# The chunk loop of a state space scan: chunks pipelined on TensorE, the skip term and the column terms of the decays as matmuls

## The reference

```python
xdt = x * dt
acs = cumsum(dt * a_neg)                       # within a chunk of 128 tokens
seg = acs[t] - acs[s]
decay_in = exp(where(tri, seg, NEG_INF))
cb = einsum('bctgn,bcsgn->bctsg', cc, bc)
y_diag = einsum('bctsg,bctsgh,bcsghp->bctghp', cb, decay_in, xdt)
states = einsum('bcsgn,bcsgh,bcsghp->bcghpn', bc, decay_out, xdt)
...
y_off = einsum('bctgn,bcghpn,bctgh->bctghp', cc, prev, exp(acs))
...
y = y_fwd + y_bwd + d_skip * xs
y = y * silu(z)
```

## Time and profile before

| | us |
|---|---|
| median of 3 runs | 2483.04 (2482.91 to 2487.15) |
| the profiled execution | 2485.22 |
| its span (first to last instruction) | 2483.4 |
| TensorE matmuls busy | 2426.9 (98%) |
| VectorE busy | 1375.8 (55%) |
| ScalarE busy | 998.4 (40%) |
| GpSimd busy | 1263.1 (51%) |

### The profile page before, as it was taken

The page is one execution under the profiler, slowest core; times in us unless marked ns, Lnnn a source line. Parts: engine busy times, 40 slices in busy tenths (PEclk is TensorE's granted clock), DMA queues, the critical chain, the costliest instruction groups (busy, mean ns, idle before and its releaser), DMA issues.

```text
span 2483.4 us, 33046 instructions
## 1 busy us (share of the span) xinstructions
PE 2426.9 (98%) x12882; PEld 2072.2 (83%) x12882; DVE 1375.8 (55%) x1561; ACT 998.4 (40%) x1737; POOL 1263.1 (51%) x814
## 2 busy tenths in 40 slices
PE   7999999999999999999999999998999999999999
PEld 6989997887888888887898899977878888888887
DVE  4476557738655546428345765586385555544332
ACT  4345567613444344212024465585144344431110
POOL 3242113323977877666633311142349877866664
PEclk9999999999999999999999999999999999999999
DMA  4434444231222212654333334442212222226544
GB/s 160 136 114 125 134 139 149 81 119 68 85 79 91 85 68 85 217 178 132 130 121 94 110 128 151 134 136 90 89 64 102 85 70 100 83 90 201 174 141 142
DMA packets 102964, 290.68 MB, mean 117 GB/s; under 512 B 7800, under 2 KB 30328, under 8 KB 101112
## 3 DMA queue, kind: packets, MB, share of 16 engines
q1 hardware_dynamic: 80360, 255.73, 30.4%
q10 hardware_dynamic: 22456, 32.90, 4.1%
HBM read 229.84 MB, written 58.75 MB: 116 GB/s over the span
## 4 chain that ended last, share of the span: by engine, by line
PE 81%; DVE 9%; ACT 4%; POOL 3%; issue 2%; DMA 1%; SPq 0%; ACTq 0%; DVEq 0%; POOLq 0%
PE PS L690 20%; PE PS L694 20%; PE PS L693 20%; PE PS L775 3%; PE PS L779 3%; PE PS L778 3%; PE PS L945 2%; PE PS L934 2%; POOL WL L629 2%; DVE HL L1780 1%; PE PS L1116 1%; PE PS L1081 1%; PE PS L924 1%; PE PS L923 1%; ACT LG L1501 1%
## 5 line engine op out<-in xcount | busy, mean ns | idle before, releaser
L605 POOL CAST WH<-RAW 128x1024 fp32r<-128x1024 f32 x156 | 184.5, 1182 | 905.5 <-PE PS L690 327.1
L690 PE MATMUL PS<-HH,WH 128*128 128x512 f32 x1264 | 496.4, 393 | 3.6 <-ACT QS L1668 2.6
L694 PE MATMUL PS<-HH,WL 128*128 128x512 f32 x1264 | 493.3, 390 | 0.0
L693 PE MATMUL PS<-HL,WH 128*128 128x512 f32 x1104 | 430.5, 390 | 0.0
L607 POOL TENSOR_TENSOR WL<-RAW,WH 128x1024 fp32r<-128x1024 f32 x156 | 396.8, 2543 | 12.5
L690 PEld LDWEIGHTS PS<-HH,WH 128*128 128x128 f32 x1264 | 237.4, 188 | 56.5 <-DVE HL L1780 3.5
L694 PEld LDWEIGHTS PS<-HH,WL 128*128 128x128 f32 x1264 | 237.3, 188 | 51.9
L690 PE MATMUL PS<-AR,WH 128*128 128x512 f32 x704 | 276.0, 392 | 2.3 <-DVE X L2208 1.8
L694 PE MATMUL PS<-AR,WL 128*128 128x512 f32 x704 | 275.9, 392 | 0.0
L693 PE MATMUL PS<-AR,WH 128*128 128x512 f32 x704 | 275.2, 391 | 0.0
L775 PE MATMUL PS<-WH,HH 128*128 128x256 f32 (+1 forms) x896 | 261.0, 291 | 1.7 <-ACT KN L1307 1.3
(11 more groups left out here) (274 smaller groups left out, 4677.3 us busy)
## 6 DMA issues: line engine op xcount, KB each, us to landing
RAW<-wst SPq DMA_DIRECT2D x156, 512.0 KB, 3.5
TOE<-toe_d SPq DMA_DIRECT2D x64, 512.0 KB, 3.7
act_d<-CVV SPq DMA_DIRECT2D x22, 1024.0 KB, 4.0
ARL<-act_d SPq DMA_DIRECT2D x88, 256.0 KB, 3.3
RAW<-wst SPq DMA_DIRECT2D x20, 1024.0 KB, 4.9
RAWB<-wst SPq DMA_DIRECT2D x20, 1024.0 KB, 4.9
XBS<-xbc_d SPq DMA_DIRECT2D x24, 512.0 KB, 4.2
xbc_d<-CV ACTq DMA_DIRECT2D x16, 512.0 KB, 3.6
```

What stands on the lines that cost most here:

```text
L605: nc.gpsimd.tensor_copy(hi, raw).then_inc(hi_done, 1)
L690: ins = nc.tensor.matmul(out, wh, xh, start=first, stop=False, skip_group_check=onto)
L693: nc.tensor.matmul(out, wh, xl, start=False, stop=False, skip_group_check=onto)
L694: return nc.tensor.matmul(out, wl, xh, start=False, stop=last, skip_group_check=onto)
```

## The change

- The chunks are pipelined one step further on TensorE. The order for chunk `c` is now: state product of `c`; sums 2 and 3 of `c`; the skip products of `c` (new); `chunk_turn` of `c + 1`; sums 0 and 1 of `c + 1`; outer products of `c + 1`; the MLP's products of `c + 1`; masked products of `c`. `BC` has two buffers.
- The skip term is made by TensorE: four matmuls of the x columns by a diagonal matrix `DIAG`, 128 columns each, which open the accumulation in bank 4 that the masked products continue. GpSimd keeps `XW` and one addition, `Y3 = Y1 + Y2`.
- The column terms are added by TensorE: a third matmul of 512 columns in each `sums`, `NRM` times `SID` with the inner axis repeated 128 times. ScalarE's exponentials have no bias and 512 columns, four in a chunk.
- `NRM` comes from four more matmuls in the backward pass (`bias_rows`), a copy by ScalarE at step `i == 3` and a subtraction by VectorE in `far()`, which also makes `DIAG` and `SID`.
- The scaling of `ST` for chunk 0 stands ahead of ScalarE's loop, that of chunk `c + 1` inside chunk `c`.
- VectorE's order for chunk `c`: add to the state, decays, `Y1`, state decay and MLP gate of `c + 1`, then the output of `c`. It waits for GpSimd's `Y3` of the chunk before it writes `Y1`.

```diff
@@ gpsimd: scan
-                    pool.wait_ge(chunk_done, 1 + n)
-                    step.then(nc.gpsimd.tensor_tensor(by_head(Y3[:]), xs, per_head(par_("d_skip")), ALU.mult))
-                    if c < LINKS:
+                    if 0 < c < LINKS:
+                        pool.wait_ge(yz_ready, 2 + n)
+                        pool.wait_ge(y12_done, 1 + l * LINKS + c)
                         pool.wait_ge(y2_ready, l * LINKS + c + 1)
-                        ins = nc.gpsimd.tensor_tensor(Y3[:], Y3[:], Y2[:], ALU.add)
...
-                        ins = nc.gpsimd.tensor_tensor(Y3[:], Y3[:], Y1[:], ALU.add)
-                    ins.then_inc(y3_ready, 1)
+                        nc.gpsimd.tensor_tensor(Y3[:], Y1[:], Y2[:], ALU.add).then_inc(y3_ready, 1)
@@ tensor: backward pass
+                def bias_rows():
+
+                    pe.wait_ge(att_done, (l + 1) * NT)
+                    for part in range(2):
+                        for low in range(2):
+                            last = nc.tensor.matmul(PS[low * 64:low * 64 + 64, 7, (2 + part) * P:(3 + part) * P],
+                                                    NACS[:].rearrange("p c e -> p (c e)")[:, part * 64:part * 64 + 64],
+                                                    ident, start=True, stop=True, skip_group_check=True)
+                    last.then_inc(rows_full, 1)
...
                     ra_state(i - 1)
+                    if i == 2:
+                        bias_rows()
@@ tensor: sums
                         nc.tensor.matmul(bank(2 + j % 2), SEL[:, rows:rows + 1].to_broadcast((P, P)),
-                                         MHL[:, part].rearrange("p h n -> p (h n)"), start=False, stop=True,
-                                         skip_group_check=True).then_inc(ab_full, 1)
+                                         MHL[:, part].rearrange("p h n -> p (h n)"), start=False, stop=False,
+                                         skip_group_check=True)
+                        nc.tensor.matmul(bank(2 + j % 2), NRM[:, part],
+                                         SID[:, 4 * rows:4 * rows + 4].unsqueeze(2).to_broadcast((P, 4, P)),
+                                         start=False, stop=True, skip_group_check=True).then_inc(ab_full, 1)
@@ tensor: chunk
+                def chunk(c):
+                    n, par, end = l * NT + c, c % 2, c == NT - 1
+
                     if not end:
                         pe.wait_ge(bst_ready, n + 1)
                         pe.wait_ge(xw_ready, l * LINKS + c + 1)
                         pe.wait_ge(gt_done, n + 1)
                         for g in range(GROUPS):
-                            last = nc.tensor.matmul(PS[:, 7, g * 256:(g + 1) * 256], BC[:, 0, g, :],
+                            last = nc.tensor.matmul(PS[:, 7, g * 256:(g + 1) * 256], BC[:, par, 0, g, :],
                                                     XW[:, g * 256:(g + 1) * 256], start=True, stop=True)
                         last.then_inc(sf_full, 1)
+                    sums(n, 2)
+                    sums(n, 3)
+                    pe.wait_ge(chunk_done, 1 + n)
+                    for j in range(4):
+                        last = nc.tensor.matmul(PS[:, 4, j * P:(j + 1) * P], XBS[:, par, j, :], DIAG[:, j], start=(j == 0),
+                                                stop=False, skip_group_check=True)
+                    last.then_inc(xbs_used, 1)
+                    if not end:
+                        pe.wait_ge(xbs_full[1 - par], 16 * (l * 6 + 2 + c // 2 + par + 1))
+                        pe.wait_ge(bst_ready, n + 1)
+                        chunk_turn(c // 2, 1 - par)
                         sums(n + 1, 0)
                         sums(n + 1, 1)
+                        outer(c + 1)
+                        mixed(c + 1)
...
-                                                    XS[:, par, e * HD:(e + 1) * HD], start=True, stop=True)
+                                                    XS[:, par, e * HD:(e + 1) * HD], start=False, stop=True,
+                                                    skip_group_check=True)
@@ scalar
+                    if i == 3:
+                        act.wait_ge(rows_full, 2 * l + 2)
+                        A(NRM[:].rearrange("p a n -> p (a n)"), PS[:, 7, 2 * P:4 * P], ACT.Copy).then_inc(far_step, 1)
...
+                v_scaled(0)
...
-                        for h in range(4):
-                            e = d * 8 + g * 4 + h
-                            last = A(SEG[par][:, j, h, :], PS[:, 2 + j % 2, h * P:(h + 1) * P], ACT.Exp,
-                                     bias=NACS[:, c, e:e + 1])
-                        last.then_inc(exp_ready, 1)
-                        if j == 1:
-                            v_scaled(c)
+                        A(SEG[par][:, j].rearrange("p h n -> p (h n)"), bank(2 + j % 2), ACT.Exp).then_inc(exp_ready, 1)
+                        if j == 1 and c < LINKS:
+                            v_scaled(c + 1)
@@ vector: far
+                    TT(DIAG[:].rearrange("p j (a e) -> p j a e", a=2),
+                       ident.rearrange("p (a e) -> p a e", a=2).unsqueeze(1).to_broadcast((P, 4, 2, HD)),
+                       par_("d_skip").rearrange("p (j a) -> p j a", a=2).unsqueeze(3).to_broadcast((P, 4, 2, HD)), ALU.mult)
...
+                    TT(SID[:], ident[:, 0:64], ident[:, 64:P], ALU.add)
+                    TT(NRM[64:P].rearrange("p a n -> p (a n)"), PS[64:P, 7, 2 * P:4 * P],
+                       NRM[64:P].rearrange("p a n -> p (a n)").bitcast(F32), ALU.subtract)
@@ vector: the chunk loop
+                def outer_parts(c):
...
+                        if c >= 2:
+                            dve.wait_ge(y3_ready, l * (LINKS - 1) + c - 1)
+                        TT(by_head(Y1[:]), by_head(bank(5)), heads(EACS, c), ALU.mult).then_inc(y12_done, 1)
...
+                outer_parts(0)
+                for c in range(NT):
+                    if c < LINKS:
+                        state_sum(c)
+                    masked(c)
+                    if c < LINKS:
+                        outer_parts(c + 1)
+                    else:
+                        y_inverse(0, NT - 1)
+                        normalise(0)
+                        normalise(1)
+                    gated_out(c)
```

More of the change, by code:

```diff
@@ L268, in trunk @@
         ZG = place("ZG", [P, 2, 3, UC], u_at + 8192)
+        DIAG = place("DIAG", [P, 4, P], u_at + 29952)
+        NRM = place("NRM", [P, 2, P], u_at + 24576, F32R)
+        SID = place("SID", [P, 64], u_at + 25600, F32R)
         JUNK = place("JUNK", [P, GROUPS, 256], u_at + 16384)
@@ L294, in trunk @@
         XS = work("XS", [P, 2, INNER])
-        BC = work("BC", [P, 2, GROUPS, P])
+        BC = place("BC", [P, 2, 2, GROUPS, P], u_at + 25856)
         XW = work("XW", [P, INNER])
@@ L591, in _ @@
             pool.sem_inc(w_ready, 2)
-            step = Steps(pool, p_step)
             def split(u, s, skipped):
@@ L1064, in sums, with outer @@
                         nc.tensor.matmul(bank(2 + j % 2), SEL[:, rows:rows + 1].to_broadcast((P, P)),
-                                         MHL[:, part].rearrange("p h n -> p (h n)"), start=False, stop=True,
-                                         skip_group_check=True).then_inc(ab_full, 1)
-                def chunk(i2, par, end):
-                    c = i2 * 2 + par
-                    n = l * NT + c
+                                         MHL[:, part].rearrange("p h n -> p (h n)"), start=False, stop=False,
[3 more added lines that the diff above has]
+                                         start=False, stop=True, skip_group_check=True).then_inc(ab_full, 1)
+                def outer(c):
+                    n, par = l * NT + c, c % 2
                     if c:
@@ L1074, in chunk @@
                         pe.wait_ge(y12_done, 1 + l * LINKS + c - 1)
-                    if not end:
+                    if c < LINKS:
                         pe.wait_ge(y2_ready, l * LINKS + c)
-                    for d in range(0 if c else 1, 1 if end else 2):
+                    for d in range(0 if c else 1, 2 if c < LINKS else 1):
                         for g in range(GROUPS):
@@ L1127, in _ @@
                 pe.wait_ge(ra_done, 1 + (l + 1) * LINKS)
+                outer(0)
+                mixed(0)
                 for c in range(NT):
-                    chunk(c // 2, c % 2, c == NT - 1)
+                    chunk(c)
                 def y_turn(c):
@@ new lines, in by_head, with heads @@
+                def by_head(t):
+                    return t.rearrange("p (h e) -> p h e", h=HEADS)
+                def heads(t, c):
+                    return t[:, c, 0:8].unsqueeze(2).to_broadcast((P, HEADS, HD))
+                def outer_parts(c):
+                    n, par = l * NT + c, c % 2
+                    if c:
+                        dve.wait_ge(yo_full, n + 1)
+                        if c >= 2:
+                            dve.wait_ge(y3_ready, l * (LINKS - 1) + c - 1)
```

(33 more changed lines are left out.)

77 lines of the change are left out of this document (11 added, 66 removed).

## The result

The changed kernel takes 2514.13 us (median of 4 runs, 2512.92 to 2515.7), the kernel before 2484.72: the ratio is 1.0112 [1.01, 1.0124], 29.4 us slower where 24.5 were forecast (2507.5 against 2483.04). The profiled execution has a span of 2512.1 us, 28.7 above the 2483.4 of before.

The account below looks back on a forecast made before the run. The prediction took TensorE to bound the kernel: start 2.5, middle 8.2 and end 1.9 us make 12.6 a layer, 25 for two. On the median of 2483.04 that gave 2508, stated as 2507.5, range 2495 to 2520 us.

Parts of the forecast that it names:

- TensorE is the bound: Middle chunks of the loop: TensorE's own work sets the period, 8.35 us without waits before, 10.15 with the added matmuls.
- Rival (a): TensorE, middle chunks: gaps between weight loads can be filled, period 9.42, whole time 2499.5 us; chance 0.14.
- The new order holds that pace: Middle chunks: the new order runs at 10.15 us; thinnest cover, 0.4 us, at VectorE's wait for Y3, costed at nothing.
- rival (b): Middle chunks: a GpSimd-VectorE crossing delays the MLP gate and TensorE waits, 7 to 12 us more, 2518; chance 0.15.
- What it takes off ScalarE buys only 0.44 us a chunk: Middle chunks: ScalarE gains 2.1 us a chunk, but only 0.44 of TensorE waiting can be returned.
- Rival (c): Middle chunks: ScalarE's exponentials set the pace, added matmuls fit idle time, 8.35 us or less, 2477 in all; chance 0.07.
- Start of the loop, +2.5: Up to the outer products of chunk 1: constants, longer first sums and later copies add 2.5 us a layer (1.5 to 3.5).
- End of the loop, +1.9: After chunk 7's outer products: the output comes later, +1.9 us a layer, +0.5 to +3 depending on the clock.
- passes it on: Output projection behind the loop: filled TensorE work that hands on the loop's delay, 12.6 us a layer.
- The sum: Both layers: 2.5 + 8.2 + 1.9 = 12.6 us a layer, 25 for two.
- the small terms are more often hidden than not: Whole kernel: reason given for saying 2507.5 us rather than the 2508 reached on the median.
- the middle's lower bound: Chunks 1 to 7: least growth at the matmuls' lowest price, 6.8 us a layer, where 8.2 was forecast.

Follow-up runs that it names:

- e12: Changed kernel with only the third matmul of each sums removed (column terms left out, all constants still made): 2500.72 us, ratio 1.0059.
- e2: Changed kernel with the skip term back on GpSimd, no DIAG and no skip products; order and third matmuls stay: 2506.98 us, ratio 1.0085.
- e8: Kernel before, in its old order, with only the column terms summed by TensorE and exponentials of 512 columns: 2513.2 us, ratio 1.011.
- e11: Changed kernel with the skip term back on GpSimd and no third matmul in the sums (column terms left out), exponentials still wide: ratio 1.0088.
- before: The kernel without the change, old chunk order and nothing added: 2484.72 us.
- e4: Changed kernel with useless matmuls into a free bank in TensorE's gaps at the end of the loop: 2507.8 us, ratio 1.0087.
- after: The changed kernel, new chunk order with both skip products and column terms on TensorE: 2514.13 us, ratio 1.0112.
- e9: Kernel before, in its old order, with only the skip term made by TensorE: 2491.0 us, ratio 1.0026.

## Why the prediction came out as it did

- **TensorE is the bound.** Right. The middle grew by 7.76 us in layer 0 and 8.65 in layer 1, 16.4 in all, forecast 2 x 8.2. The period is 10.09, forecast 10.15: matmuls at 0.215 instead of 0.23, skip products 0.89 for 0.90. Rival (a), room hidden in the weight loads with a period of 9.42, is out: loads are busy for 55.87 of 60.45 us, and yet TensorE had nothing to give. The rule of the Trainium skill (Perfetto Trace Analysis, Identifying the Most-Contended Engine) that this share, beside the achieved share of peak, measures the headroom doesn't hold here: loads stood at 92% and TensorE was full. e12's 0.215 us a matmul follows the moving columns.
- **The new order holds that pace.** Right, event by event: `Y2` ends 9.18 us after the outer products (9.3), GpSimd's `Y3` at 10.70 (10.6 to 11.1), the gate 3.67 (3.75), and the state product, wanted at 4.2 (4.31 by the prediction's own layout), started at 4.46 unhindered. VectorE's `Y1` waits for the outer products, not for `Y3`:

```profile
439.91 0.69 DVE L2169 TENSOR_TENSOR Y<-PS,EACS 128x512 f32<-128x512 f32 x1 [2.44 <-PE PS L1091]
440.52 0.68 DVE L2171 TENSOR_TENSOR CURF<-CURF,CDEC 128x512 f32<-128x512 f32 x1
441.23 0.42 DVE L2174 TENSOR_TENSOR YT<-PS,ZG 128x256 f32<-128x256 f32 x1
```

  So rival (b)'s cover held. But (b)'s price was well judged only because the skip term had left GpSimd: in e2, e8 and e11 the same crossings appear.
- **What it takes off ScalarE buys only 0.44 us a chunk.** Right for the sum (ScalarE is 13.65 us less busy in the middle, 12 forecast). Rival (c) is out: no run in the old order returned time by it, and e8 paid for it.
- **Start of the loop, +2.5.** Right in size: +2.65. In its parts, 1.96 came ahead of the first sums (1.55 forecast) and 0.69 behind them (0.95). `bias_rows` is the 0.66 of L1022 at 393.48, forecast 0.4; `DIAG`, `SID` and `NRM` are 0.64, 0.22 and 0.43 long on VectorE, 1.29 for a forecast of 1.15. Two errors of 0.3 to 0.4 us cancel here.

```profile
401.65 0.64 DVE L2101 TENSOR_TENSOR DIAG<-CST,PARM 128x512 f32<-128x512 f32 x1
...
402.48 0.22 DVE L2107 TENSOR_TENSOR SID<-CST 128x64 fp32r<-128x64 f32 x1
402.71 0.43 DVE L2108 TENSOR_TENSOR NRM<-PS,NRM 64x256 fp32r<-64x256 f32 x1
```

- **End of the loop, +1.9.** This term was too small. In layer 0 the tail grew by 2.65 and the first products of the projection ran at half clock, which cost another 1.43: 4.1 in all, above even the bound of 3. The sentence that failed is that the projection "passes it on": it was counted as filled work at full rate, as before had it there. In layer 1 the tail grew by 1.10 only, since before's own tail was longer there: its last masked products waited 2.67 us, not 1.43, and its projection started at a granted clock of 0.57 as well.

```profile
1697.88 3.65 PE L1116 MATMUL PS<-XS,SEG 128*128 128x64 f32 x16 [2.67 <-DVE SEG L2144]
```

- **The sum.** Unrounded, the forecast was 25.2 us for two layers. Against it stand, in the spans, 5.4 for the starts (5.0; of the 4.14 between the layers 1.43 is the projection, and in layer 1 TensorE's first sums ran slow, 0.42 from one start to the next at 1648.43, 0.21 in layer 0), 16.4 for the middles (16.4), 5.2 for the ends (3.8), the 1.95 ahead of the changed code, which e4 shows to vary between executions, and -0.2 behind: 28.7. The prediction then took 0.7 off because "the small terms are more often hidden than not", and this went the wrong way. Three smaller sums in it are off and bear on nothing: by its own prices the middle's lower bound is 7.1 and not 6.8, and rival (c)'s terms give 4.1 us a layer, 2475, and not 3; the third is the 4.2 above.
- **What the prediction didn't ask.** It costed the additions and took the order as given. The order alone costs 23 us, by a loop that the wide exponentials then shorten (10.08 to 9.38, below TensorE's 10.09) and by its longer end. This changed no term of the sum, but read as a list of prices (additions some 21 us, order some 4) the prediction would have misled anyone who wanted to undo a part.

## What to carry to other kernels

Where one engine's starts follow each other without a wait, count what a change adds to that engine, in starts of like rows; here it gave the middle to 0.4 us in 8. When parts are to be judged one by one, lay out the loop through all engines for each combination: the column terms cost 27 us alone and 21 together with the skip term, since alone they moved GpSimd's work onto VectorE's. Relieving an engine that doesn't set the pace can cost time, and the stretch behind the loop has to be costed at the clock that the gaps in front of it leave.

## What the runs showed of the hardware

- A useless matmul can pay: with TensorE's gaps filled its granted clock stayed at 1.00 (e4). In after it fell within the eight masked products at 486.57 (1.44 us for 1.10), behind waits of 0.93 and 0.16, stood at 1.00 again behind one of 1.44 (492.52), and was at 0.50 (1.2 GHz) from 494.45, behind one of 0.83, into the projection: 3.1 us of filled work in layer 0 and 4.4 in layer 1. What the waits alone don't settle is the level at which the projection starts: before, with waits of 1.43, 0.73, 0.82 and 1.21 us, starts it at 1.00 in layer 0 and at 0.57 in layer 1.
- Crossings can lock in. A 128x512 VectorE operation takes 0.69 us alone and up to 1.77 when it starts while a GpSimd one runs (e2, e8, e11); GpSimd's addition takes 1.26 alone (before, 421.47) and up to 1.80 crossed (e11). In these traces the one that starts second is stretched: in before GpSimd started 0.19 us first and VectorE took 1.65; in e9 VectorE started first, at 446.24, and took 0.69, and GpSimd's, begun 0.07 us later, took 1.76. In e8 this repeats in every chunk, in before in every second. The Trainium skill (Perfetto Trace Analysis, Optimizing Scalar/DVE Operations) has the two engines share a read port. The runs agree, and whether a crossing repeats in every period is what decides its price.
- Matmuls of 512 columns of the reduced fp32 kind start 0.21 to 0.24 us apart; the first one behind full fp32 matmuls takes 0.41 (after, 443.18 to 443.59), behind B times C 0.31 (446.63 to 446.94).
